# Second attention's opening: an exchange ahead of a high half and a rotation ahead of maxima; third block's last steps: low halves of probabilities ahead of taps

## What is computed

```python
def windowed_gqa(h, w_qkv, w_o, sinks, cos, sin):          # "second attention"
    q, k, v = jnp.split(h @ w_qkv, [Hq * d, Hq * d + Hkv * d], axis=-1)
    q = apply_rope(q, cos, sin); k = apply_rope(k, cos, sin)
    s = einsum('bnqhgd,bnchd->bnhgqc', q, band(k)) * d ** -0.5     # |i-j| <= 128
    m = maximum(max(s), sink); e = exp(s - m)
    pr = e / (sum(e) + exp(sink - m))
    return einsum('bnhgqc,bnchd->bnqhgd', pr, band(v)) @ w_o

def second_block(x, ...):                                   # "third block" of the kernel
    a = a_in[..., :512] * sigmoid(a_in[..., 512:])
    a = causal_depthwise_conv(a, w_dw, b_dw)                 # 31 taps
    q, k = rmsnorm(q, g_q), rmsnorm(k, g_k)                  # per head
    s = q @ k.T * scale + c[:, None] - c[None, :]            # causal, forgetting bias
    y_attn = (softmax(s) @ v) @ w_attn_out
    x = x + (sigmoid(gate_a) * y_conv + sigmoid(gate_b) * y_attn) @ w_out
```

## Time and profile before

| | us |
|---|---|
| median of 3 runs | 2097.93 |
| lowest, highest | 2096.63, 2098.93 |
| profiled execution, as timed | 2095.74 |
| its span, first to last instruction | 2094.0 |
| TensorE busy in the span | 2043.6 (98%) |
| VectorE busy | 1226.8 (59%) |
| ScalarE busy | 942.3 (45%) |
| GpSimd busy | 905.9 (43%) |

### The profile page before, as it was taken

One profiled execution on the slowest core, in us unless ns is written; L12 is line 12 of the kernel. 1 busy time (PEld: TensorE's weight loads), 2 busy tenths in 40 slices (PEclk: granted clock), 3 DMA queues, 4 the chain that ended last, 5 costly groups with the idle time before them and its releaser, 6 DMA issues.

```text
span 2094.0 us, 28726 instructions
## 1 busy us (share of the span) xinstructions
PE 2043.6 (98%) x9976; PEld 1683.2 (80%) x9976; DVE 1226.8 (59%) x1842; ACT 942.3 (45%) x1494; POOL 905.9 (43%) x660
## 2 busy tenths in 40 slices
PE   6999999999999989899999999999999999999999
PEld 5777788888887878788888887878888788888887
DVE  7487867646275679856636267538879473213222
ACT  5456545434245467644524245434742544323222
POOL 4322135554446431144545446444215454455454
PEclk9999899999999999999999999999999999999999
DMA  4322122322223210022332323222003222232323
GB/s 148 101 76 76 41 81 91 109 93 96 97 98 112 90 61 32 31 81 91 100 102 91 100 92 119 91 81 88 34 31 101 85 97 90 90 104 97 101 90 111
DMA packets 52612, 183.21 MB, mean 87 GB/s; under 512 B 6432, under 2 KB 6688, under 8 KB 52512
## 3 DMA queue, kind: packets, MB, share of 16 engines
q1 hardware_dynamic: 51072, 177.76, 25.8%
q10 hardware_dynamic: 1440, 4.07, 0.5%
HBM read 176.04 MB, written 2.10 MB: 85 GB/s over the span
## 4 chain that ended last, share of the span: by engine, by line
PE 58%; issue 23%; POOL 14%; DVE 4%; ACT 1%; POOLq 0%; DVEq 0%; ACTq 0%
PE PS L530 56%; POOL wlo L522 14%; PE PS L759 1%; DVE acc L1597 0%; DVE AR L1760 0%; DVE ptlo L1768 0%; DVE AR L2234 0%; DVE nmax L1716 0%; DVE Blo L2238 0%; ACT Bhi L1100 0%; DVE Blo L1590 0%; DVE X L1633 0%; DVE AR L2232 0%; ACT AR L1171 0%; DVE qklo L1706 0%
## 5 line engine op out<-in xcount | busy, mean ns | idle before, releaser
L522 POOL TENSOR_TENSOR wlo<-raw,whi 128x512 fp32r<-128x512 f32 x656 | 905.7, 1404 | 1174.9 <-ACT whi L1074 1173.8
L530 PE MATMUL PS<-Bhi,whi 128*128 128x512 f32 x2368 | 935.0, 395 | 24.7 <-POOL wlo L522 15.4
L530 PE MATMUL PS<-Blo,whi 128*128 128x512 f32 x2368 | 924.1, 390 | 0.0
L530 PE MATMUL PS<-Bhi,wlo 128*128 128x512 f32 x2368 | 923.9, 390 | 0.0
L1074 ACT ACTIVATE whi<-raw 128x1024 fp32r<-128x1024 f32 x328 | 345.4, 1056 | 515.4 <-PE PS L530 445.9
L530 PEld LDWEIGHTS PS<-Bhi,whi 128*128 128x128 f32 x2368 | 445.5, 188 | 134.5 <-issue 30.2
L530 PEld LDWEIGHTS PS<-Bhi,wlo 128*128 128x128 f32 x2368 | 445.8, 188 | 94.2
L530 PEld LDWEIGHTS PS<-Blo,whi 128*128 128x128 f32 x2368 | 446.0, 188 | 89.8 <-issue 0.5
L1581 DVE TENSOR_TENSOR AR<-PS,R 128x512 f32<-128x512 f32 x170 | 115.3, 689 | 236.2 <-PE PS L530 224.7
L1633 DVE TENSOR_TENSOR X<-X,PS 128x512 f32<-128x512 f32 x88 | 60.3, 687 | 227.0 <-PE PS L530 226.3
L1878 DVE SCALAR_TENSOR_TENSOR AR<-AR,par_sb 128x511 f32<-128x511 f32 x88 | 117.6, 1336 | 8.8 <-ACT AR L1307 8.8
(11 more groups left out here) (230 smaller groups left out, 2030.2 us busy)
## 6 DMA issues: line engine op xcount, KB each, us to landing
raw<-in_weights SPq DMA_DIRECT2D x328, 512.0 KB, 3.2
AR<-AR SPq DMA_DIRECT2D x56, 64.0 KB, 2.0
X<-in_xT ACTq DMA_DIRECT2D x4, 512.0 KB, 7.7
out<-X SPq DMA_DIRECT2D x8, 256.0 KB, 3.1
AR<-in_pT ACTq DMA_DIRECT2D x2, 512.0 KB, 3.9
par_sb<-in_parameters ACTq DMA_DIRECT2D x1, 322.0 KB, 4.5
AR<-in_positions ACTq DMA_DIRECT2D x1, 256.0 KB, 9.0
con_sb<-in_constants ACTq DMA_DIRECT2D x1, 198.5 KB, 8.9
```

The source lines that it names most:

```text
L522: ins = pool.tensor_tensor(wlo[:, j, c], raw[:, j % RAWS, c], f32(whi[:, j, c]), ALU.subtract)
L530: return pe.matmul(out, w, x, start=start, stop=stop)
```

## The change

Three things are moved, and nothing is added or removed. In the opening of the second attention ScalarE does `swap_halves` of projection 1 ahead of `q_high` of projection 0, and in step 0 VectorE does `rope(1)` ahead of `maxima(2)`. In the steps of the third block that have no projection piece (8 to 15), VectorE does `prob_low(g)` straight behind `normalise(g+1)`, ahead of the second group of taps and of `head_norm`.

```diff
--- before.py
+++ after.py
@@ -1424,8 +1424,8 @@
             values("v2", (0,), 0, 256)
             exps(2, 0)
             swap_halves("kq2", 0, QT0[2] + 2)
+            swap_halves("kq2", 1, QT0[2] + 3)
             q_high(*place_of(2, 0))
-            swap_halves("kq2", 1, QT0[2] + 3)
             attention(2)
             output_high(OA, 7)
             residual("o2", "ffn1")
@@ -1819,13 +1819,15 @@
                     begun, halfway = finished(kind, g - 1), finished(kind, g - 2)
                     if kind == 3 and g and halfway is not None:
                         head_inverse(halfway)
+                    if kind == 2 and g == 0:
+                        rope(PROJ[kind], begun, place_of(kind, begun)[0])
                     if g + AHEAD[kind] < steps:
                         maxima(kind, g + AHEAD[kind])
                     if kind == 3 and begun is not None:
                         head_scaled(begun)
                     if kind == 3:
                         taps(1)
-                    if kind == 2 and begun is not None:
+                    if kind == 2 and g and begun is not None:
                         rope(PROJ[kind], begun, place_of(kind, begun)[0])
                     if kind < 3 and halfway is not None:
                         q_low(*place_of(kind, halfway))
@@ -1836,11 +1838,14 @@
                         normalise(kind, g + 1)
                     if kind == 1 and begun is not None:
                         rope_add(begun)
+                    if kind == 3 and piece(3, g) is None:
+                        prob_low(kind, g)
                     if kind == 3:
                         taps(TAPS_A_STEP[g % 4] - 1)
                         if g and halfway is not None:
                             head_norm(halfway)
-                    prob_low(kind, g)
+                    if kind < 3 or piece(3, g) is not None:
+                        prob_low(kind, g)
                     if kind == 3 and halfway is not None:
                         head_low(halfway)
                     if kind == 1 and finished(1, g) is not None:
```

## The result

| | before | after |
|---|---|---|
| median, 20 runs of each side by side | 2095.13 | 2100.06 |
| ratio, with its 95% interval | | 1.0025 (1.0018 to 1.0031) |
| mean granted clock of TensorE over the timed runs | 0.993 | 0.991 |
| span of the profiled execution | 2094.0 | 2098.7 |

The changed kernel is slower by 0.25%, 4.9 us by the medians, 3.8 to 6.5 us by the interval.

The account below looks back on a forecast made before the run. TensorE works almost throughout, so only its waits can be won, and VectorE stands behind them. Opening 0 + 2.4 and third block -0.4 gave +2.0 on the median 2097.93: 2099.9 us, range 2094.8 to 2102.0.

Parts of the forecast that it names:

- Opening, first step: Second attention's opening: the exchange runs 1.3 us earlier, so projection 2 starts 1.34 us sooner for TensorE, here only.
- Opening, what is late next: GpSimd's pair delays normalise(1) by 2.0 us; step 2's transposes stand where they stood, so the opening gains nothing at full clock.
- Opening, the clock: Behind TensorE's sparse stretch in the opening the clock falls to 0.50 for 4 to 6 us of work: +2.4 us.
- Third block: Steps 8 to 15: step 10's transposes come 1.9 us sooner, two new waits follow, step 11 is unmoved: -0.4 us.
- No clock fall (1): Port collision in the opening but no fall of the clock: opening 0, third block -0.4, 2097.5 us; chance 0.12.
- no collision (2): GpSimd's pair misses normalise(1) in the opening: 2.1 us won there, 0.4 in the third block, 2095.4 us; chance 0.25.
- kept no clock (3): Third block keeps its clock or regains it sooner: 1.5 us won there rather than 0.4, 2098.8 us; chance 0.09.
- The fourth: Opening at half clock for 10 us, third block's gate matmuls under low clock 1.7 us more: 2104 us; chance 0.04.

Follow-up runs that it names:

- filled opening: The opening's two moves, third block as before, plus 12 unread 128x512 matrix products ahead of the transposes of step 1, against the kernel before: 2097.77 us, ratio 1.0018.
- opening only: The changed kernel without the third block's edit, so only the opening's two moves, against the kernel before: 2100.33 us, ratio 1.0023.
- later high half: The opening's two moves, with the first weight slab's high half moved into step 1 behind exps(2), against the kernel before: 2098.99 us, ratio 1.0014.
- rotation only: The kernel before with only VectorE's rope(1) moved ahead of maxima(2): 2100.01 us, ratio 1.0023.
- exchange only: The kernel before with only ScalarE's swap_halves of projection 1 moved ahead of q_high of projection 0: 2095.41 us, ratio 1.0002.
- third block only: The kernel before with only the third block's move of prob_low: 2094.64 us, ratio 0.9999.
- head_norm first: The third block's edit alone, with head_norm(g-2) ahead of prob_low(g) in steps 8 to 15, against the kernel before: 2095.54 us, ratio 1.0002.
- filled kernel before: The kernel before plus unread 128x384 products in waits of the second attention's last eight steps and before the third block's step 10 transposes: 2091.97 us, ratio 0.9981.
- kernel before with its end filled: The kernel before, nothing moved, plus unread 128x384 products in TensorE's waits at the end of the second attention: 2094.17 us, ratio 0.9990.

## Why the prediction was right and wrong

- **Opening, first step: right.** With 1.32 us taken off, exchange forecast at 756.13 and found there, projection 2 at 759.40 and found there.
- **Opening, what is late next: right.** GpSimd's pair forecast at 762.73, found 762.63; two TENSOR_SCALARs forecast at 2.7 us, found 2.57; transposes of step 1 forecast 766.08, found 765.93; scores(2,4) forecast 768.05, found 767.89. The filled opening shows its sum, nothing at full clock, though not its last step: the second pair was to miss normalise(2), and with the clock at 1.00 it didn't (1.78 us); that cost TensorE 0.28 us. The rule of the Trainium skill (SBUF — State Buffer, "Who interferes with whom") holds in the rows shown here: TENSOR_SCALARs and TENSOR_TENSORs with two inputs in SBUF are stretched under a pair of GpSimd, prob_low and the reductions, which read PSUM, are not.
- **Opening, the clock: the fall was right, the size of the term was not.** It fell where forecast (766 to 773). In the opening it costs 1.6 to 1.8 us (forecast 2.4). The step that failed is the sentence behind it: "After this TensorE is the one that is waited for, so the loss stays." It does stay through twenty steps (82.8 us in all kernels), but at the end of the second attention, where the clock swings too, another 3.4 us come up in the profile, and in the timed runs 5.1 less 1.0, 4.1 us, by the medians and 4.8 less 2.5, 2.3 us, by the ratios, with intervals of about 2 us to each side. The prediction had looked for the clock only where instructions moved, and its sum has no term for the end. The term was 2.4; it measured 1.8 in the opening, and 2 to 4 more came at the end.
- **Third block: the waits right, its sign not seen.** VectorE idle 0.79 us (0.8 forecast), step 11 at its old distance; -0.4 forecast, ratio 0.9999 measured (0.9988 to 1.0010), which cannot tell 0.4 us from nothing. The 0.6 us that the changed kernel is longer from 3,0 to the end stands in the profile of the opening only too, so it isn't this edit's.
- **The rivals.** No clock fall (1) is out; no collision (2) did not come by 0.25 us, a margin that the prediction gave as 0.17. In its numbers 767.35 is the end of q_low(1), where 767.58 and 768.64 are starts; its sum holds. The third block kept no clock (3). The fourth named a longer low clock in the opening (10 us; it was 6.8) and under the gates, and these are not where the loss lay, though the first gate matmuls did run at 0.51.
- **The total.** +2.0 forecast, +4.9 measured. 2099.9 stands beside 2100.06 because the base, 2097.93 of three runs, was 2.8 above the median of twenty. Slower by over 0.2% had been given 6 in 100 and is what the ratio says, by 0.05%; its interval reaches below that bound.

What the low stretch at the end costs is plain from the profiles. In the 12 us from the start of the transposes of step 31 the granted clock is 0.72 in the changed kernel, in the opening only, and in that with the later high half; it is 0.86 in the rotation only and in the exchange only, and 0.96 to 1.00 in the kernel before, the third block only, head_norm first, and the opening filled. The stage 2,31 to 3,0 is 580.2 us in the first three, 578.7 in the next two and 576.8 to 577.7 in the rest. 12 x 0.28 = 3.4 and 12 x 0.14 = 1.7: the stage is longer by what the clock took there. A window of the exchange only, at the first matmuls behind the last outputs' wait:

```profile
893.00:897.00 4.00, 4.00 (x21) 3.87 (x21) 0.63 (x2) 0.56 (x1) 0.00 (x0) 0.61 0.01 4
```

What stays open is why the stretch falls there. The first three kernels and the rotation only have a low stretch in the opening too; the exchange only has none there and yet has the bad place at the end, in an execution of 2097.77 us, 2.4 above that kernel's median. So the opening's stretch goes with the bad place but is not needed for it, and not all that sets it. That it shifts the program against instants at which the clock changes is my reading; it was not shown. Nor is it shown where the opening filled loses its 2.9 us: its profiled execution lacks both the opening's stretch and the bad place.

## What to carry to other kernels

Cost a moved instruction at full clock first, and then ask of every place behind it, not only the edited one, whether TensorE's clock swings there and what lies under its low stretch: here, by the profiles, more than half of the loss lay 130 us behind the edit. Where an engine that paces the kernel has runs of short waits, unread matrix products in them were worth more (47 of them 2.9 us of 2095, the 35 at the end of the second attention alone 1.4) than any of the three reorderings. A wait removed on one engine's queue is only worth what is late next: here one collision moved by one step, and one wait of 2.34 us became waits of 0.44, 1.47 and 1.46.

## What the runs showed of the hardware that was not expected

- The same instructions and the same wait (2.35 us, 0.68 to 0.71 us busy in 3) left the clock at 1.00 in the kernel before and were followed by a low stretch in the filled kernel before. So one profile of such a place does not say what the next execution does.
- A low stretch can end in a gain: it delayed GpSimd's second pair past normalise(2), and the opening became 1.4 us shorter.
- A 128x2 TENSOR_TENSOR of VectorE with both inputs in SBUF, 0.15 us alone, takes up to 1.27 us when it meets GpSimd's pair (1.14, 1.19, 1.23 and 1.27, but also 0.38 with the later high half and 0.78 in the changed kernel). A RECIPROCAL of 128x2 beside it stays at 0.17.
- Unread products at 128x384 ended the low stretches at the end of the second attention altogether (clock 1.00 from 862 to 900 in the kernel before with its end filled, 0.81 in 862 to 880 before), and cost nothing that shows. With the opening's moves the same products left one of them (0.79 in 868 to 876).
